# A software pipeline's order changed in the attention stage of a two-layer hybrid trunk: maxima ahead of the previous step's normalise, turns two steps late around the gates' blocks

## What is computed

```
def attend(q, k, v, scale):
    ...
    def block(qblk):
        s = jnp.einsum('bqgrd,bkgd->bgrqk', qblk.astype(jnp.float32), kf) * scale
        p = jax.nn.softmax(s, axis=-1)
        return jnp.einsum('bgrqk,bkgv->bqgrv', p, vf)
...
y_a = attend(aq..., ak, av, A_HEAD_DIM ** -0.5)
o1 = attend(cq[:, :, :, 0:1], ck[:, :, :, 0], cv, C_HEAD_DIM ** -0.5)
o2 = attend(cq[:, :, :, 1:2], ck[:, :, :, 1], cv, C_HEAD_DIM ** -0.5)
y_c = rms_norm((o1 - lam * o2)[:, :, :, 0], p['c_subln_g']) * (1.0 - lam_init)
...
gates = jax.nn.sigmoid(merge_logits.reshape(bsz, t, N_BRANCH, D_MODEL))
mixed = jnp.sum(gates * proj, axis=2) @ p['w_out']
```

## Time and profile before

| | us |
|---|---|
| median of 3 runs | 2565.3 |
| lowest and highest | 2562.66, 2570.05 |
| the profiled execution | 2566.29 |
| its span in the profile | 2564.5 |
| TensorE matmul busy over the span | 2447.3 (95%) |
| TensorE weight loads busy | 2287.8 (89%) |
| VectorE busy | 1363.9 (53%) |
| ScalarE busy | 928.4 (36%) |
| attention stage of layer 0, first scores to last weigh | 290.2 to 440.1 |
| attention stage of layer 1 | 1540.6 to 1691.4 |

### The profile page before, as it was taken

One profiled execution on the slowest core, in us unless ns is written; L12 is line 12 of the kernel. 1 busy time (PEld: TensorE's weight loads), 2 busy tenths in 40 slices (PEclk: granted clock), 3 DMA queues, 4 the chain that ended last, 5 costly groups with the idle time before them and its releaser, 6 DMA issues.

```text
span 2564.5 us, 50362 instructions
## 1 busy us (share of the span) xinstructions
PE 2447.3 (95%) x22010; PEld 2287.8 (89%) x22010; DVE 1363.9 (53%) x2104; ACT 928.4 (36%) x1294; POOL 2.2 (0%) x6
## 2 busy tenths in 40 slices
PE   5999998999999999999989999979999999999998
PEld 4899776888999999999989997768899989999998
DVE  4134466886754555553241436668775654554621
ACT  4245564322143433342143545542222443333410
POOL 0000000000000000000000000000000000000000
PEclk8999997999999999999999999989999999999999
DMA  8654111222244222223344421112222622222221
GB/s 274 203 164 148 37 45 32 53 53 53 62 149 132 68 81 75 72 62 87 84 140 140 132 82 34 53 32 52 55 64 77 210 57 82 67 82 60 68 75 68
DMA packets 323606, 228.52 MB, mean 89 GB/s; under 512 B 17952, under 2 KB 317024, under 8 KB 322656
## 3 DMA queue, kind: packets, MB, share of 16 engines
q1 hardware_dynamic: 317584, 211.32, 28.2%
q10 hardware_dynamic: 5840, 14.51, 1.7%
HBM read 215.44 MB, written 10.35 MB: 88 GB/s over the span
## 4 chain that ended last, share of the span: by engine, by line
PE 83%; DVE 11%; issue 3%; ACT 2%; DMA 1%; SPq 0%; DVEq 0%; ACTq 0%
PE PS L703 21%; PE PS L704 21%; PE PS L705 21%; DVE RING_split L1788 2%; PE PS L913 2%; PE PS L928 2%; PE PS L944 2%; PE PS L880 1%; PE PS L727 1%; PE PS L1023 1%; DVE BIG L1976 1%; PE PS L821 1%; PE PS L882 1%; PE PS L881 1%; PE PS L823 1%
## 5 line engine op out<-in xcount | busy, mean ns | idle before, releaser
L703 PE MATMUL PS<-HH_split,WHI_split 128*128 128x320 f32 x3168 | 995.9, 314 | 19.1 <-DVE HL_split L1763 8.6
L705 PE MATMUL PS<-HH_split,RING_split 128*128 128x320 f32 x3136 | 973.1, 310 | 0.0
L704 PE MATMUL PS<-HL_split,WHI_split 128*128 128x320 f32 x2912 | 905.3, 311 | 0.0
L703 PEld LDWEIGHTS PS<-HH_split,WHI_split 128*128 128x128 f32 x3168 | 599.8, 189 | 32.2 <-issue 23.3
L705 PEld LDWEIGHTS PS<-HH_split,RING_split 128*128 128x128 f32 x3136 | 592.8, 189 | 0.0
L704 PEld LDWEIGHTS PS<-HL_split,WHI_split 128*128 128x128 f32 x2912 | 552.1, 190 | 0.3
L1788 DVE TENSOR_TENSOR RING_split<-RING,WHI_split 128x1024 fp32r<-128x1024 f32 (+2 forms) x204 | 274.8, 1348 | 473.7 <-ACT WHI_split L1520 235.7
L704 PE MATMUL PS<-ZT_split,WHI_split 128*128 128x320 f32 x1216 | 376.9, 310 | 0.0
L704 PEld LDWEIGHTS PS<-ZT_split,WHI_split 128*128 128x128 f32 x1216 | 229.1, 188 | 0.0
L1520 ACT ACTIVATE WHI_split<-RING 128x1024 fp32r<-128x1024 f32 x88 | 93.3, 1060 | 290.3 <-PE PS L705 290.3
L1795 DVE TENSOR_TENSOR RING_split<-RING,WHI_split 128x1024 fp32r<-128x1024 f32 x52 | 62.3, 1223 | 234.9 <-ACT WHI_split L1245 234.8
(11 more groups left out here) (234 smaller groups left out, 3293.8 us busy)
## 6 DMA issues: line engine op xcount, KB each, us to landing
RING<-in_w_in SPq DMA_DIRECT2D x96, 512.0 KB, 4.1
RING<-in_w_up SPq DMA_DIRECT2D x88, 512.0 KB, 5.0
RING<-in_w_ada SPq DMA_DIRECT2D x80, 512.0 KB, 6.3
RING<-in_w_down SPq DMA_DIRECT2D x32, 384.0 KB, 3.4
RING<-in_w_in SPq DMA_DIRECT2D x40, 256.0 KB, 3.4
RING<-in_w_down SPq DMA_DIRECT2D x32, 320.0 KB, 3.9
RING<-in_w_out SPq DMA_DIRECT2D x16, 512.0 KB, 4.6
ZT<-in_w_ada SPq DMA_DIRECT2D x8, 1024.0 KB, 9.9
```

The source lines that it names most:

```text
L703: release(pe.matmul(out, w_hi, hi[:, a:b], start=begin, stop=False), fresh and a == 0)
L704: pe.matmul(out, w_hi, lo[:, a:b], start=False, stop=False)
L705: ins = pe.matmul(out, w_lo, hi[:, a:b], start=False, stop=end)
```

## The change

Nothing is computed otherwise; three loops are written in another order.

- TensorE: `turn(g - 1, 0)` goes, `turn(g - 2, 0)` comes, right behind the scores. The first helping of gates now stands between the two turns of a matrix pair, and weigh behind the second.
- ScalarE: the copy of the first turn moves from behind the exponentials of the step before to ahead of the exponentials; the copy of the second moves from ahead of them to behind them.
- VectorE: `maxima(g)` moves ahead of `outputs` and `normalise(g - 1)`. `early_lo` stays first in the loop body.

```diff
@@ TensorE
                 for g in range(NG + 3):
                     if g < NG:
                         scores(g)
+                    turn(g - 2, 0)
+                    gate_fill(g, 0)
                     turn(g - 2, 1)
                     weigh(g - 3)
-                    gate_fill(g, 0)
-                    turn(g - 1, 0)
                     gate_fill(g, 1)
@@ ScalarE
                 for g in range(NG + 3):
                     gates_kept(halves_before(g))
-                    keep_turned(g - 2, 1)
+                    keep_turned(g - 2, 0)
                     if g < NG:
                         exponentials(g)
-                    keep_turned(g - 1, 0)
+                    keep_turned(g - 2, 1)
                 gates_kept(2 * N_EARLY)
@@ VectorE
                     while early < N_EARLY and 2 * early <= halves_before(g - 1):
                         early_lo(early)
                         early += 1
+                    if g < NG:
+                        maxima(g)
                     if g % NS == 5:
                         outputs(g // NS, 0)
                     if g > NS and g % NS == 3:
                         outputs(g // NS - 1, 1)
                     if g:
                         normalise(g - 1)
-                    if g < NG:
-                        maxima(g)
```

## The result

The changed kernel took 2615.0 us (median; 2608.65 to 2621.47 over four runs) against 2565.9 (median; 2562.66 to 2570.05) for the kernel before: a ratio of 1.0189 with a 95% interval of 1.0167 to 1.0211, so 49 us slower. The forecast was 2602, with a range of 2583 to 2618. The four runs lie in two pairs, 2609 us at a mean granted clock of 0.973 and 2621 at 0.966; the profiled one is of the second pair (2621.47, span 2619.6).

A forecast was written before the change was run, and what follows sets the result against it. The prediction took the attention stage to be bound by TensorE's own work. Its terms, 16.2 + 4.8 + 3.4 + 4 + 8 = 36.4 us on the profiled 2566.3, an execution 1.0 above the median, gave 2602 (range 2583 to 2618).

The forecast's parts named there:

- `early_lo` behind a normalise: Steps 2, 6, 10, 14, 18: TensorE's gates wait for `early_lo`, now queued behind a normalise; 8.1 us a layer, 16.2 in all.
- Both turns in one step: Steps 8, 9, 20, 21: second turn waits for ScalarE's copy of the first; 0.6 us each, 4.8 in all.
- The copy ahead of the exponentials: ScalarE, every step: first turn's copy delays the exponentials, floor of 5.03 us a step; 3.4 us in all.
- The context steps: From step 24 on, without gates: an added turn, copy waits and normalises in a row; 2 us a layer, 4 in all.
- The clock: TensorE falls to half clock after idle time, five falls of eight places, 1.6 us each; 8 us.
- The upper bound of 13: Upper bound of the half-clock term, with all eight places falling: 13 us.
- the sum's own upper end of 2611: Whole kernel: forecast time with the terms' upper bounds, +46 us, 2611.
- the fourth rival: Clock falls wherever TensorE now waits: all eight places, two-turn steps, steps 22 and 23, context steps; +54, 2619 us; 14%.
- The first: Rival: TensorE had room, the exponentials loop set the steps; floor of 5.03 us for all 24, 2544 us; 2%.
- The second: Rival: no change, TensorE's work only dealt out otherwise and `early_lo` not on its path; 2565 us; 4%.
- the third: Rival: only the `early_lo` term is real, copies find slack, clock holds, context steps break even; 2581 us; 8%.
- What was to be seen: Signs in the profile after: listed waits, step floor, half-clock spells; both attention stages grow by 14 to 22 us, nothing else.

The follow-up runs named there:

- e1: Changed kernel with VectorE's `early_lo` (L1788) put back directly behind the maxima, ahead of the normalise: 2585.2 us, ratio 1.0071 to the kernel before.
- e5: e1 with weigh put between the two turns of a step on TensorE: 2579.8 us, ratio 1.0048.
- e4b: Changed kernel with identity matmuls ahead of the gates in TensorE's idle time, 7 in step 2 and 11 in steps 6, 10, 18: 2597.9 us.
- e7: Kernel before, its loops unchanged, with the last 16 blocks of gates spread over steps 18 to 23 instead of 18 to 21: 2557.2 us, ratio 0.9961.
- e3: Kernel before with TensorE's and ScalarE's part of the change alone; VectorE keeps normalise ahead of maxima: 2585.1 us, ratio 1.0074.
- e4: Changed kernel with 20 more identity matmuls ahead of the gates in steps 2, 6, 10 and 18 of both layers: 2611.9 us, ratio 1.0179.

## Why the prediction was right, and which term was mis-sized

**`early_lo` behind a normalise: right, to the tenth.** Forecast 1.86 us for steps 6, 10 and 18 and 1.27 for 2 and 14. At full clock (third column) they are 1.84 or 1.85 and 1.26, 8.1 a layer and 16.1 in all. e1 undoes it in steps 2, 6, 10 and 18; in step 14 a second wait comes to light, as told below.

**Both turns in one step: right, a little small.** Forecast 0.6 for each of steps 8, 9, 20 and 21 with 0.75 as the bound; measured 0.74 and 0.73, so 2.9 a layer instead of 2.4. The second turn starts 3.35 us into the step, as forecast, but TensorE would have been ready for it at about 2.64 and not at 2.85. From the first turn to the gates behind it are 0.63 us and not 0.8 (345.98 to 346.61), and the block takes 0.52: L882 starts 0.37 us after L880, and in the kernel before, a turn followed such an L882 by 0.15,

```profile
337.18 0.31 PE L882 MATMUL PS<-HH_split,RING_split 128*128 128x320 f32 x1
...
337.33 0.82 PE L928 MATMUL PS<-CONST,BIG 128*128 128x128 f32 x6
```

That makes a delay of 0.71. Step 14 shows the same wait once L1788 is early again (6.67 us in e1 against 5.67 before), which the expectation of e1 had left out; step 2 doesn't, as its second turn had waited for a copy in the kernel before too. What I didn't see was `outputs` behind the maxima: in the changed kernel it costs nothing, since in step 9 `outputs` ends at 354.47 and weigh starts at 354.85, and e5 laid it bare at 1.1 us in steps 9 and 21.

**The copy ahead of the exponentials: right.** Every one-turn step without L1788 takes 5.03 or 5.04 us at full clock. Steps 4, 5 and 23 answer; step 1 is 4.51 where the clock holds, 0.47 less than before.

These three make 12.64 us a layer (143.77 against 131.13 for steps 0 to 23 at full clock), 25.3 in all against 24.4 forecast.

**The context steps: right in sum.** 18.7 and 18.1 us became 21.7 and 18.9, together 3.7 against 4. The granted clock in them was 0.66 and 0.77, which goes with the spread between the layers; no run takes the two apart.

**The clock: mechanism right, size wrong by a factor of two to three.** This is the term that puts most of the 13 us between the forecast and the median: by e4b the half clock cost 17 us and not 8. I took five falls of eight and 1.6 us each, 8 in all. In the profiled execution all eight places fell, and the spells were not all of the 3.4 us seen before: in layer 0 the clock was at half for 10.2 us behind step 2, 3.4 behind step 6, 6.8 behind 10 and 3.4 behind 18, in layer 1 for 6.8, 3.4, 10.2 and 6.8. That is 51 us, eight falls of 6.4 on the mean. Steps 0 to 23 took 25.5 and 23.4 us more than before; less 25.3 for the waits that leaves 23.6 for the clock (the kernel before had one fall of 1.6 itself). In the pair of runs at 2609 us, of which there is no profile, it should be about 12 less; e4b, whose waits are the same, says 17 between the medians. The step of the working that failed is this term, in two of its factors. The number: eight falls, not five. The length: I took the one fall of the earlier trace rows, which ended while TensorE was busy, as the length of all. What a short fall costs was right: step 7 behind the 3.4 us of step 6 took 1.60 us more than at full clock. The upper bound of 13 was built on the same length and was too low as well, and with it the sum's own upper end of 2611. That the median still lies in the range is in part luck: it is owed to the fourth rival, whose falls "wherever TensorE waits" took the range up to 2618, and two of the four runs lie above that too.

**The rivals.** The first (TensorE has room; 2544) is out: with every repair the new order is level with the old, and in e7 work taken off the filled steps 19 to 21 shortened them by 1.9 us of the 2.6 that six blocks take, as it should where TensorE's work sets the length. The Trainium skill's page "Perfetto Trace Analysis", section "Identifying the Most-Contended Engine", would have TensorE's room judged by weight-load busy time, beside the share of the peak rate, and not by matmul busy time. The weight-load part of that doesn't fit this stage: 71% by it, against 94% by matmul busy time, and no run found room. The second (no change) is out by the result, and the third (`early_lo` alone, 2581) by e1 and e3, which leave 19 us without it. The fourth came nearest to the size, 2619, for half of its reasons: the eight places fell, the two-turn steps did not.

**What was to be seen.** L1788's wait of 2.6 us, a wait of 0.5 ahead of the second turn, no step under 5.0 from step 2 on (step 0 is 4.59, and step 1 4.51 in layer 1), half clock behind steps 2, 6, 10 and 18, growth only in the stages: all there. The growth was 24 to 28 us a stage, not 14 to 22.

## What to carry to other kernels

When instructions change places on an in-order engine, look first at what stood directly behind the moved one for another engine's sake: here a 1.2 us job that fed TensorE moved behind a 1.9 us one, and a line that the diff leaves untouched became the price. Idle time of 2.6 us on TensorE cost more than itself here, since the clock fell behind it and stayed low for 3.4 to 10.2 us; a repair that takes no wait away but keeps TensorE at work there gave 17 us. And in this stage, which TensorE's own work sets, another order of the waits gained nothing, but moving six blocks of that work from full steps to steps where TensorE stood idle gained 8.4 us.

## What the runs showed of the hardware that was not expected

- Half clock outlasted its cause. Behind step 2 of layer 0 TensorE was busy for 9.67 of 10 us at a granted clock of 0.51, about half of them with gates' blocks back to back; in layer 1 behind step 10, 9.18 of 10 us at 0.54. Why it ended after 3.4 us in some places and 10.2 in others is open; no run was made to settle it.
- The same idle time was followed by half clock in some places and not in others. In the changed kernel TensorE stood idle for 1.94 us ahead of step 1 in layer 0 and 1.95 in layer 1; the clock fell in layer 0 (5.84 us) and held in layer 1 (4.51). In e1 it fell in both layers (5.84 and 5.94), in the second behind two idle times of 0.92 and 1.29 us with six matmuls between them.
- A 128x128 f32 matmul of the identity took 0.22 to 0.24 us in e4 (4.73 us for the 20, each with two entries in the trace), where the transposes of a turn take 0.13 (six in 0.8). The forecast of 2.2 us for 20 had been made from the transposes.
